# Streaming encoder trunk: one more row group of the first convolution projection in rounded products, and a new order at both FFN ends

## The chip, the core and the metric

One core of a Trainium2 chip runs the whole program. The metric is the device time of one launch in microseconds (us). The engines are TensorE (PE in the profile, its weight loads PEld), VectorE (DVE), ScalarE (ACT), GpSimd (POOL) and SyncE (SP). SP only issues transfers here; POOL issues those that add while they copy.

## What is computed

256 tokens of width 2048 pass through two layers: a Conformer convolution module with a SwiGLU FFN of width 5632, then multi-head latent attention with a second FFN, then a final RMSNorm.

```python
def conv_module(h, w_pw1, b_pw1, w_dw, b_dw, ln_g, ln_b, w_pw2, b_pw2):
    u = h @ w_pw1 + b_pw1                      # 2048 -> 4096
    a, gate = jnp.split(u, 2, axis=-1)
    v = a * jax.nn.sigmoid(gate)
    v = lax.conv_general_dilated(
        v, w_dw[:, None, :].astype(v.dtype), window_strides=(1,),
        padding=[(CONV_WIDTH - 1, 0)], dimension_numbers=('NWC', 'WIO', 'NWC'),
        feature_group_count=D_MODEL) + b_dw
    v = jax.nn.silu(layernorm(v, ln_g, ln_b))
    return v @ w_pw2 + b_pw2                   # 2048 -> 2048

def swiglu(h, w_gate, w_up, w_down):
    return (jax.nn.silu(h @ w_gate) * (h @ w_up)) @ w_down

def reference(...):
    ...
        h = h + y
        h = h + swiglu(rmsnorm(h, ffn_norm_g[i]), ffn_w_gate[i], ffn_w_up[i], ffn_w_down[i])
    return rmsnorm(h, final_norm_g)
```

Here `y` is the mixer's output for `rmsnorm(h, attn_norm_g[i])`, the convolution (31 taps, one filter a channel) in layer 0 and latent attention in layer 1.

Everything is float32. The kernel gets it in one of two ways. A plain float32 product is one instruction in the code and two records in the trace. A product "in three rounded terms" splits each operand into a rounded part (`_hi`, float32r) and the remainder (`_lo`): hi*hi + hi*lo + lo*hi, three fast matmuls.

## The kernel before

**Weights.** They come from HBM in groups of 1 MB: 512 rows (4 tiles of 128) by 512 columns. `raw`, `w_hi` and `w_lo` each have `RING = 4` slots; group `g` uses slot `g % 4`. ACT writes `w_hi` (a rounding copy, `hi`). The remainder is made in one of two ways: DVE subtracts (`lo`), or ACT writes `-raw` rounded into `w_lo` (`hi_and_negative`) and POOL issues a transfer that adds `raw` onto it (`conv_low`). A `raw` slot is loaded again when its last reader is done: PE (`group_used`) for a float32 group, the remainder (`lo_dve` or `lo_added`) for a rounded one. SP issues all loads in one queue, in program order.

**First projection and convolution** (`channel_half`, `conv_half`, `gate_sigmoid`, `products`, `conv_sums`, `conv_rows`). Eight halves `s = 0..7`, each 256 channels and their gates: four row groups `j`, each 4 tiles of rows by 4 tiles of columns (16 products of 128x128 weights by 256 tokens). `WHOLE = 2`: groups 0 and 1 are float32 products from `raw` and `x_f`; groups 2 and 3 are rounded, their remainders by `conv_low`. After a half, ACT takes the sigmoid of the gates (line 723), DVE multiplies (line 1086), and the 31 taps are shared: ACT makes 10 products (741) that POOL adds up (603), DVE does 21 steps for each of two channel tiles in turn (1101), and adds both sums (1107). In the last half ACT and POOL take 5 taps, DVE 14, and PE 12 with diagonal matrices (`diag_last`, made by ACT at line 712 after the first half's operands). `conv_rows` turns a finished half back to token rows. In the last half ACT also prepares the four groups of the second projection (`G_PW2`) before and between its gate sigmoid and its products. Layer norm, SiLU (`silu`) and the second projection (`square`) follow.

**FFN** (`ffn`). Eleven chunks of 512 hidden channels; from chunk 1 on a chunk has 15 groups of 1 MB, named `Q1 Q3 Q5 D0 D1 Q6 D2 Q7 D3 Q2 G2 Q4 G3 U2 U3` in this order, each with a position `q`. The `Q` groups are Strassen-like sums for half of gate and up, `G` and `U` plain ones, `D0..D3` the down projection of the chunk before. The last chunk's four down groups are `F_LAST + n`. `f_w(q)` names the `w_hi`/`w_lo` slot: `q % 4`, and `n` for `F_LAST + n`; `f_hi` on ACT waits until PE has used the group that had the slot last. With `F_LAST = 158` slot 0 was last used by position 156 and slot 1 by 157, before as after.

```python
            def f_hi(l, q):
                landed = 16 * (F_LAYER[f_raw(q), f_sum(q)] * l + F_LOADED[q])
                act.wait_ge(f_added[f_raw(q)] if f_sum(q) else f_in[f_raw(q)], landed)
                before = f_before(q, f_w)
                if before is not None:
                    wait_f_used(act, l, before)
```

At the end of a chunk DVE multiplies gate (`gate_mul`, 1258) and up (`up_mul`, 1268) into `ff_h`; PE transposes it (`hidden`, 1719); ACT and DVE split it (830, 1250) into `a_hi`, `a_lo`; then the down groups of that chunk may start. In all chunks but the last, that chain lies beside the next chunk's `Q` groups. Every engine works through its own list in order, so an instruction that waits holds up all that stand behind it.

Of the kernel before, what the change touches and what calls it, by code (L numbers as in the profile page):

```python
# [52 lines left out]
PE_TAPS_LAST = 12  # L53

# [5 lines left out]
WHOLE = 2  # L60
SPLIT = KG - WHOLE

# [16 lines left out]

G_ADDED = G_PW2 + RING  # L80
# [18 lines left out]
DOWN = (D0, D1, D2, D3)  # L99
F_CHUNK = 15  # L100
# [3 lines left out]
F_RAW = {Q1: 0, Q5: 0, Q6: 0, Q4: 0, Q3: 1, Q7: 1, D0: 4, D1: 2, D2: 3, D3: 4, Q2: 2, G2: 3, G3: 4, U2: 2, U3: 3}  # L104


def f_pos(c, p):
    return F_FIRST + F_CHUNK * (c - 1) + p


def f_part(q):
    return (q - F_FIRST) % F_CHUNK


def f_raw(q):

    if q < F_FIRST:
        return q % RING
    return F_RAW[f_part(q)] if q < F_LAST else q - F_LAST
# [61 lines left out]
def encoder(nc, x, positions, attn_norm_g, ffn_norm_g, final_norm_g, conv_w_pw1, conv_b_pw1, conv_w_dw,  # L181
# [3 lines left out]
    with ctx:  # L185
# [137 lines left out]
        glu_done = sem("glu_done")  # L323
        conv_step = sem("conv_step")
# [59 lines left out]

        def split_no(g):

            return SPLIT * (g // KG) + g % KG - WHOLE if g < G_PW2 else SPLIT * HALVES + g - G_PW2

        def wait_lo(eng, g, i=None, per=0):
            if KG <= g < G_ADDED:  # L390
                eng.wait_ge(lo_added[g % RING], 16 * (g // KG if g % KG >= WHOLE else 1))
            else:
                eng.wait_ge(lo_dve, val(split_no(g) + 1 if g < KG else SPLIT + g - G_ADDED + 1, i, per))
# [10 lines left out]
        def wait_f_used(eng, l, q):  # L404
            eng.wait_ge(f_used, F_ALL * l + q + 1)

# [44 lines left out]
        def _(sp):  # L451
# [50 lines left out]
            def ffn_loads(l):  # L502
# [23 lines left out]
                for c in range(1, FC):  # L526
                    for p in (D3, Q2, G2):
                        part(c, p)
                    if c < FC - 1:
                        part(c + 1, Q3)  # L530
                    for p in (G3, U2, U3):
                        part(c, p)
                    if c < FC - 1:
                        part(c + 1, Q1)
                        for p in (D0, D1, D2):
                            part(c + 1, p)
                for n in range(CC):
                    f_load(F_LAST + n, w_of(l, DOWN[n], FC))
            ffn_loads(0)
# [37 lines left out]
        def _(pool):  # L577
# [9 lines left out]
            def conv_low(g):  # L587

                slot = g % RING
                pool.wait_ge(neg_done, split_no(g) - SPLIT + 1)  # L590
                pool.dma_start(hi32(w_lo[:, slot, :]), raw[:, slot, :], accum_op=ALU.add).then_inc(lo_added[slot], 16)

            def conv_sums(s):
# [3 lines left out]
                for n in range(1, PROD_TAPS[s]):  # L597
                    pool.wait_ge(prod_done, 2 * (PROD_TAP[s] + n) + 2)
# [5 lines left out]
                    if n == 2 and s < HALVES - 1:  # L604
                        conv_low(G_PW1 + KG * (s + 1) + KG - 1)
# [51 lines left out]
        def _(act):  # L657
# [51 lines left out]
            act.wait_ge(vec_done, 3)  # L709
            for mm in range(2):  # L710
                for w in range(PE_TAPS_LAST):
# [3 lines left out]
            def gate_sigmoid(s):  # L715

                u = s % 2
                act.wait_ge(group_used, G_PW1 + KG * s + KG)
                if s >= 2:
                    act.wait_ge(glu_done, 2 * (s - 1))  # L720
                for mm in range(2):
                    col = KT + 2 * s + mm
                    act.activation(glu_sig[:, 2 * u + mm, :], ps[:, 2 * u + 1, S * mm:S * mm + S], ACT.Sigmoid,
                                   bias=bias1_col[:, col:col + 1]).then_inc(glu_sig_done, 1)

            def products(s, n0, n1):

                u = s % 2
                for n in range(n0, min(n1, PROD_TAPS[s])):
                    w = prod_tap0(s) + n  # L730
                    if n == 0 and s >= 2:
                        act.wait_ge(conv_tr, TT * (s - 1))
                    elif n > 0 and PROD_ADD[s] + n > PROD_SLOTS:
                        act.wait_ge(prod_added, PROD_ADD[s] + n - PROD_SLOTS)
                    elif n > 0:
                        act.wait_ge(out_added, TT)
                    for mm in range(2):
                        m, tile = 2 * u + mm, 2 * s + mm
                        act.wait_ge(glu_done, tile + 1)
                        dst = acc[:, m, :] if n == 0 else prod_slot(s, n)[:, S * mm:S * mm + S]  # L740
                        act.activation(dst, vbuf[:, m, w:w + S], ACT.Copy, scale=tap_col[:, w, tile:tile + 1]
                                       ).then_inc(prod_done, 1)
# [9 lines left out]
            for s in range(HALVES):  # L752
                g = G_PW1 + KG * (s + 1)
                if s == HALVES - 1:
                    hi_and_negative(g)
                    hi_and_negative(g + 1)
# [57 lines left out]
            def ffn(l):  # L814

                def gate_sig(c):

                    for t in range(TT):
                        if c > 0 and t == 0:
                            act.wait_ge(tile0_done, 2 * chunk_no(l, c) + 1)  # L820
                        else:
                            wait_f_used(act, l, KG - 1 if c == 0 else f_pos(c, G3))
# [3 lines left out]
                def hidden(c):  # L826

                    for b in range(2):
                        act.wait_ge(ff_tr, 2 * (FC * l + c) + b + 1)
                        act.activation(a_hi[:, 0, 2 * b:2 * b + 2, :].rearrange("p k s -> p (k s)"), ps[:, 4 + b, :],  # L830
                                       ACT.Copy).then_inc(ahi_done, 1)

                def parts_hi(c, *parts):
                    for p in parts:
                        f_hi(l, f_pos(c, p))

# [8 lines left out]
                for c in range(1, FC):  # L845
# [4 lines left out]
                    wait_f_used(act, l, f_pos(c, Q5))  # L850
# [1134 lines left out]
```

## Time and profile before

| | us |
|---|---|
| median of 3 runs | 2071.71 (2070.03 to 2072.25) |
| time of the profiled execution | 2071.21 |
| its span on the core | 2069.4 |
| TensorE busy in the span | 2010.9 (97%) |
| mean granted TensorE clock | 0.988 |

The span is what the trace shows; 1.8 us of the profiled time lie around it. In the rows further down, a row of the timeline gives start, duration, engine, line, operation, output and inputs, count, and in brackets the idle time before it and what ended it. PE works nearly all the time, so time can go in two ways only: less work for it, or fewer of the places where it stands still or runs at the lower clock.

### The profile page before, as it was taken

Reading aid. Unit: us, or ns where it says so; the run is one execution under the profiler, and the core shown is the slowest. Engines: PE = TensorE matmul, PEld = TensorE weight load, DVE = VectorE, ACT = ScalarE, POOL = GpSimd, SP = SyncE. Lnnn points to the kernel's source line nnn. Section 1 sums busy time; section 2 is a strip of 40 time slices with the busy share of each in tenths; the row PEclk is TensorE's granted clock in tenths of the full one; section 3 lists DMA queues with packets and bytes.
Section 4 is the critical chain, followed back from the end, with each engine's and each line's share of the span. In section 5 each row is a group of like instructions: output and inputs, shape, how many; then the busy total and the mean of one; then the engine's idle time right before and its main releaser. Section 6 shows DMA issues by size and latency. Waiting matters only on the chain.

```text
span 2069.4 us, 24296 instructions
## 1 busy us (share of the span) xinstructions
PE 2010.9 (97%) x9814; PEld 1705.5 (82%) x9814; DVE 1421.9 (69%) x1605; ACT 1054.8 (51%) x1020; POOL 226.1 (11%) x191
## 2 busy tenths in 40 slices
PE   8899899999999999999989999999999999999996
PEld 7898878888888888888878998888888888888885
DVE  4777676777766777667667775477766767766764
ACT  4566763545454555455445554355455445554543
POOL 0455400000000000000001000000000000000001
PEclk9999999999999999999999999999999999999998
DMA  7888946699889989898744534568988999889981
GB/s 234 240 227 234 263 143 214 169 279 258 227 224 259 268 267 236 216 260 245 243 143 138 158 122 160 191 177 270 251 217 240 253 274 262 224 227 262 263 244 61
DMA packets 254081, 457.51 MB, mean 221 GB/s; under 512 B 18452, under 2 KB 60188, under 8 KB 251164
## 3 DMA queue, kind: packets, MB, share of 16 engines
q1 hardware_dynamic: 207648, 349.73, 48.3%
q0 software_dynamic: 44832, 102.77, 28.7%
q10 hardware_dynamic: 1500, 3.61, 0.5%
q8 instruction: 71, 1.16, 0.2%
q14 instruction: 30, 0.25, 0.0%
HBM read 435.10 MB, written 2.10 MB: 211 GB/s over the span
## 4 chain that ended last, share of the span: by engine, by line
PE 85%; DVE 5%; DMA 5%; ACT 3%; issue 1%; POOL 0%; SPq 0%; ACTq 0%; DVEq 0%; POOLq 0%
PE ps L1496 82%; DVE w_lo L988 2%; DMA raw<-in_conv_w_pw_dram 2%; DMA w_lo<-raw 1%; DMA raw<-in_ffn_w_up_dram 1%; PE ps L1719 1%; POOL scratch L603 0%; PE ps L1920 0%; PE ps L1921 0%; PE ps L1901 0%; ACT w_hi L801 0%; DMA resid<-in_x_dram 0%; ACT w_lo L677 0%; ACT diag_last L712 0%; DVE x_lo L1015 0%
## 5 line engine op out<-in xcount | busy, mean ns | idle before, releaser
L988 DVE TENSOR_TENSOR w_lo<-raw,w_hi 128x2048 fp32r<-128x2048 f32 x264 | 601.5, 2287 | 279.0 <-ACT w_hi L801 278.7
L801 ACT ACTIVATE w_hi<-raw 128x2048 fp32r<-128x2048 f32 x264 | 500.9, 1914 | 488.3 <-PE ps L1496 197.1
L1496 PE MATMUL ps<-w_hi,x_hi 128*128 128x512 f32 x1328 | 517.9, 390 | 1.1 <-DVE x_lo L1015 0.9
L1496 PE MATMUL ps<-w_hi,x_lo 128*128 128x512 f32 x1328 | 516.7, 389 | 0.0
L1496 PE MATMUL ps<-w_lo,x_hi 128*128 128x512 f32 x1328 | 516.7, 389 | 0.0
L1496 PE MATMUL ps<-w_hi,a_hi 128*128 128x512 f32 (+1 forms) x768 | 294.5, 384 | 2.5 <-DVE a_lo L1250 2.5
L1496 PE MATMUL ps<-w_lo,a_hi 128*128 128x512 f32 (+1 forms) x768 | 293.9, 383 | 0.0
L1496 PEld LDWEIGHTS ps<-w_hi,x_hi 128*128 128x128 f32 x1328 | 249.3, 188 | 53.9 <-DVE x_lo L1015 1.4
L1496 PE MATMUL ps<-w_hi,a_lo 128*128 128x512 f32 (+1 forms) x768 | 293.6, 382 | 0.0
L1496 PEld LDWEIGHTS ps<-w_hi,x_lo 128*128 128x128 f32 x1328 | 249.3, 188 | 52.1
L1496 PEld LDWEIGHTS ps<-w_lo,x_hi 128*128 128x128 f32 x1328 | 249.3, 188 | 51.3
L622 POOL DMA_DIRECT2D raw<-in_ffn_w_up_dram x60 | 77.1, 1285 | 1255.1 <-DVE w_lo L988 1255.1
L672 ACT ACTIVATE w_hi<-raw 128x2048 fp32r<-128x2048 f32 x73 | 138.5, 1910 | 147.8 <-PE ps L1496 74.3
L1496 PEld LDWEIGHTS ps<-w_hi,a_hi 128*128 128x128 f32 x768 | 145.6, 190 | 31.7 <-DVE w_lo L988 3.5
L1496 PEld LDWEIGHTS ps<-w_hi,a_lo 128*128 128x128 f32 x768 | 145.6, 190 | 28.0
L1496 PEld LDWEIGHTS ps<-w_lo,a_hi 128*128 128x128 f32 x768 | 145.6, 190 | 27.7
L801 ACT ACTIVATE w_hi<-row_bc 128x2048 fp32r<-128x2048 f32 x60 | 115.2, 1919 | 92.7 <-PE ps L1496 92.7
L983 DVE TENSOR_TENSOR w_lo<-raw,w_hi 128x2048 fp32r<-128x2048 f32 x55 | 125.5, 2291 | 40.8 <-ACT w_hi L672 40.6
L988 DVE TENSOR_TENSOR w_lo<-row_bc,w_hi 128x2048 fp32r<-128x2048 f32 x60 | 137.0, 2284 | 4.6 <-ACT w_hi L801 4.5
L1496 PE MATMUL ps<-w_hi,s_hi 128*128 128x512 f32 x320 | 126.4, 395 | 0.0
L1496 PE MATMUL ps<-w_hi,s_lo 128*128 128x512 f32 x320 | 124.8, 390 | 0.0
L1496 PE MATMUL ps<-w_lo,s_hi 128*128 128x512 f32 x320 | 124.5, 389 | 0.0
(210 smaller groups left out, 2323.8 us busy)
## 6 DMA issues: line engine op xcount, KB each, us to landing
raw<-in_ffn_w_gate_dram SPq DMA_DIRECT2D x68, 1024.0 KB, 9.5
raw<-in_ffn_w_up_dram SPq DMA_DIRECT2D x68, 1024.0 KB, 7.5
raw<-in_ffn_w_up_dram POOLq DMA_DIRECT2D x60, 1024.0 KB, 9.0
raw<-in_ffn_w_down_dram SPq DMA_DIRECT2D x48, 1024.0 KB, 6.0
row_bc<-in_ffn_w_down_dram SPq DMA_DIRECT2D x40, 1024.0 KB, 8.8
raw<-in_conv_w_pw_dram SPq DMA_DIRECT2D x64, 512.0 KB
raw<-in_ffn_w_gate_dram POOLq DMA_DIRECT2D x20, 1024.0 KB, 9.8
row_bc<-in_ffn_w_gate_dram SPq DMA_DIRECT2D x20, 1024.0 KB, 6.4
```

What stands on the lines that cost most here:

```text
L622: pool.dma_start(f_raw_tile(l, q).rearrange("p (k n) -> p k n", k=GK), w_of(l, p, c), accum_op=ALU.add).then_inc(f_added[f_raw(q)], 16)
L672: act.activation(w_hi[:, slot, :], raw[:, slot, :], ACT.Copy).then_inc(hi_done, 1)
L801: act.activation(f_w_tile(w_hi, l, q), f_raw_tile(l, q), ACT.Copy).then_inc(f_hi_done, 1)
L983: dve.tensor_tensor(w_lo[:, g % RING, :], raw[:, g % RING, :], hi32(w_hi[:, g % RING, :]), ALU.subtract).then_inc(lo_dve, 1)
L988: dve.tensor_tensor(f_w_tile(w_lo, l, q), f_raw_tile(l, q), hi32(f_w_tile(w_hi, l, q)), ALU.subtract).then_inc(f_lo_done, 1)
L1496: ins = pe.matmul(dst, lhsT, rhs, start=first and n == 0, stop=last and n == len(pairs) - 1, skip_group_check=skip)
L1719: ins = pe.transpose(ps[:, 4 + b, S * kk + P * t:S * kk + P * t + P], ff_h[:, t, P * m:P * m + P], ident[:, :])
```

## The change

1. `WHOLE` goes from 2 to 1: row group 1 of each half is rounded too. Its remainder is made by DVE (`lo`), right after the half's two gate multiplications; groups 2 and 3 keep `conv_low` (`ADDED_FROM = 2`). The second projection's first four groups (`G_PW2 + 0..3`) get their remainders by DVE too, one before the SiLU steps and three between them.
2. The load of group 1 no longer waits for PE's use of it but for its remainder. ACT prepares group 1, then group 2, takes the sigmoids, and then prepares group 3 ahead of its products; POOL issues both adding transfers ahead of its sums. `diag_last` is made four matrices at a time after the products of halves 1 to 6. ACT loads its Sigmoid table early.
3. In the last half PE finishes channel tile 0 and its gates (`last_tile0`), then tile 1; ACT and DVE take tile 0, then tile 1, in that order.
4. In the last FFN chunk the order is `Q6 Q2 Q7 G2 G3 Q4 U2 U3 D2 D3`: two down groups of the chunk before come last, and `hidden` stands between them. SP's order follows. `a_hi`/`a_lo` of the last chunk use another slot and the transposes other PSUM banks.

```diff
-WHOLE = 2
+WHOLE = 1
+ADDED_FROM = 2
+ORDER_LAST = (Q1, Q3, Q5, D0, D1, Q6, Q2, Q7, G2, G3, Q4, U2, U3, D2, D3)
...
             for s in range(HALVES):
-                if s == HALVES - 1:
-                    for j in range(WHOLE):
-                        conv_low(G_PW2 + j)
-                    conv_low(G_PW2 + WHOLE)
-                else:
-                    conv_low(G_PW1 + KG * (s + 1) + WHOLE)
+                if s < HALVES - 1:
+                    for j in range(ADDED_FROM, KG):
+                        conv_low(G_PW1 + KG * (s + 1) + j)
                 conv_sums(s)
-            conv_low(G_PW2 + KG - 1)
...
+            for s in range(HALVES - 1):
                 g = G_PW1 + KG * (s + 1)
+                hi(g + 1)
                 hi_and_negative(g + 2)
-                gate_sigmoid(s)
+                for mm in range(2):
+                    gate_sigmoid(s, mm)
+                hi_and_negative(g + 3)
                 products(s, 0, 3)
-                hi_and_negative(g + 3)
                 if s > 0:
                     rows_out(s - 1)
-                products(s, 3, TAPS)
+                products(s, 3, PROD_TAPS[s])
+                if s > 0:
+                    last_diagonals(s - 1)
+            for mm in range(2):
+                gate_sigmoid(HALVES - 1, mm)
+                for n in range(PROD_TAPS[HALVES - 1]):
+                    product_of(HALVES - 1, n, mm)
+                if mm == 0:
+                    hi(G_PW2)
+            rows_out(HALVES - 2)
+            for j in range(1, KG):
+                hi(G_PW2 + j)
             rows_out(HALVES - 1)
...
@@ DVE, conv_half @@
+                if last:
                     for mm in range(2):
+                        gated(mm)
+                        for w in range(w0, TAPS):
+                            tap(w, mm)
+                else:
+                    gated(0)
+                    gated(1)
+                    lo(G_PW1 + KG * (s + 1) + WHOLE)
+                    for w in range(w0, TAPS):
+                        tap(w, 0)
+                        tap(w, 1)
...
@@ PE, channel_half @@
+                    elif j == ADDED_FROM:
+                        channel_products(s, j, (0, 2))
+                    else:
+                        channel_products(s, j, (0, 2)).then_inc(last_tile0, 1)
+                        channel_products(s, ADDED_FROM, (1, 3)).then_inc(group_used, 1)
+                        channel_products(s, j, (1, 3)).then_inc(group_used, 1)
...
@@ SP, last chunk of the FFN @@
+                c = FC - 1
+                for p in (G2, G3, U2):
+                    part(c, p)
+                last_down(1)
+                part(c, U3)
+                last_down(0)
+                part(c, D2)
+                part(c, D3)
+                last_down(2)
+                last_down(3)
...
@@ ACT, last chunk @@
+                        parts_hi(c, Q6, Q2, Q7, G2)
+                        q167_out(c)
+                        parts_hi(c, G3, Q4, U2, U3)
+                        gate_sig(c)
+                        parts_hi(c, D2, D3)
+                        f_hi(l, f_next(c, 0))
...
+                    f_hi(l, f_next(c, 1))
+                    if c < FC - 1:
+                        f_hi(l, f_next(c, 2))
                 hidden(FC - 1)
...
@@ DVE, last chunk @@
+                        parts_lo(c, G3, Q4, U2, U3)
+                        gate_mul(c)
+                        parts_lo(c, D2, D3)
+                        f_lo(l, f_next(c, 0))
+                        up_mul(c)
+                        f_lo(l, f_next(c, 1))
+                        hidden(c)
+                        add(2, f_pos(c, D2))
+                        f_lo(l, f_next(c, 2))
+                        add(3, f_pos(c, D3))
+                        f_lo(l, f_next(c, 3))
...
@@ PE, last chunk @@
+                        q2(c)
+                        q7(c)
...
+                        plain(c, G2, 0, 2, q167_done)
+                        plain(c, G3, 0, 3)
+                        strassen(c, Q4, 1, x_tile(1, 1))
+                        pe.wait_ge(mixed, 4 * n + 4)
                     plain(c, U2, 2, 2)
                     plain(c, U3, 2, 3)
+                    if c == FC - 1:
+                        down(c - 1, 2, f_pos(c, D2))
+                        hidden(c)
+                        down(c - 1, 3, f_pos(c, D3))
```

`f_next(c, n)` is the position `n` places after the end of chunk `c`; behind the last chunk that is `F_LAST + n`. `q7` waits for the second of DVE's three mixing steps (lines 1301 to 1306), which itself needs `Q6` done by PE.

## Rows read from the trace of the kernel before

**Rows 1.** The page, part 1: busy us, share of the span, instructions.
```profile
PE 2010.9 (97%) x9814; PEld 1705.5 (82%) x9814; DVE 1421.9 (69%) x1605; ACT 1054.8 (51%) x1020; POOL 226.1 (11%) x191
```
**Rows 2.** The chain that ended last, in time order: start us, us, what.
```profile
42.21 3.31 ACT diag_last L712 x11
...
57.95 11.41 DMA w_lo<-raw
...
230.17 18.50 DMA raw<-in_conv_w_pw_dram
...
1040.47 1.92 ACT w_hi L801
```
**Rows 3.** Timeline of PE, an undisturbed half of the projection.
```profile
84.76 7.07 PE L1496 MATMUL ps<-x_f,raw 128*128 128x256 f32 x32
...
91.79 0.28 PE L1496 MATMUL ps<-x_lo,w_hi 128*128 128x256 f32 x1
...
103.05 0.28 PE L1496 MATMUL ps<-x_hi,w_lo 128*128 128x256 f32 x1
```
**Rows 4.** Timeline of PE, the two longest stops of the projection.
```profile
69.40 0.58 PE L1496 MATMUL ps<-x_hi,w_hi 128*128 128x256 f32 x1 [4.82 <-DMA w_lo<-raw]
...
77.41 0.81 PE L1496 MATMUL ps<-x_f,raw 128*128 128x256 f32 x3
...
203.85 0.43 PE L1496 MATMUL ps<-x_hi,w_hi 128*128 128x256 f32 x1 [1.97 <-DMA w_lo<-raw]
```
**Rows 5.** Busy by stretch, core 0: no transfer, an adding one alone, loads alone.
```profile
104.00:106.00 2.00, 2.00 (x11) 1.74 (x11) 0.00 (x0) 2.00 (x2) 0.00 (x0) 1.00 0.04 14
...
110.00:112.00 2.00, 2.00 (x13) 1.77 (x12) 2.00 (x7) 2.00 (x3) 1.86 (x2) 1.00 1.00 197
126.00:128.00 2.00, 2.00 (x20) 2.00 (x18) 0.51 (x2) 0.00 (x0) 0.00 (x0) 1.00 1.11 349
```
**Rows 6.** Transfers issued in 100 to 164 us: KB, median us to landing.
```profile
w_lo<-raw POOLq DMA_DIRECT2D x5, 1024.0 KB, 8.2
```
**Rows 7.** Timelines of ACT and of DVE in the same halves.
```profile
129.75 1.91 ACT L672 ACTIVATE w_hi<-raw 128x2048 fp32r<-128x2048 f32 x1 [9.47 <-DMA raw<-in_conv_w_pw_dram]
...
108.78 15.76 DVE L1101 SCALAR_TENSOR_TENSOR ps<-scratch,tap_col,ps 128x256 f32<-128x256 f32 x40
```
**Rows 8.** Timelines behind the last half: PE, then DVE, then ACT.
```profile
241.21 12.58 PE L1496 MATMUL ps<-diag_last,scratch 128*128 128x128 f32 x96 [3.65 <-DVE scratch L1086]
257.32 1.16 PE L1496 MATMUL ps<-ident,scratch 128*128 128x128 f32 x8 [3.53 <-DVE scratch L1107]
...
269.90 0.47 PE L1496 MATMUL ps<-w_hi,x_hi 128*128 128x512 f32 x1 [0.20 <-DVE x_lo L1152]
...
242.27 10.27 DVE L1101 SCALAR_TENSOR_TENSOR ps<-scratch,tap_col,ps 128x256 f32<-128x256 f32 x26
256.52 0.75 DVE L1107 TENSOR_TENSOR scratch<-scratch,ps 128x256 f32<-128x256 f32 x2 [3.98 <-POOL scratch L603]
...
248.69 1.91 ACT L672 ACTIVATE w_hi<-raw 128x2048 fp32r<-128x2048 f32 x1 [5.03 <-DMA raw<-in_conv_w_pw_dram]
```
**Rows 9.** Timelines at the first FFN's end: PE, then ACT, then DVE.
```profile
1046.08 1.97 PE L1719 MATMUL ps<-ident,scratch 128*128 128x128 f32 x8 [5.71 <-DVE scratch L1268]
1048.97 0.77 PE L1496 MATMUL ps<-w_hi,a_hi 128*128 128x512 f32 x1 [0.92 <-DVE a_lo L1250]
...
1054.11 0.40 PE L1496 MATMUL ps<-w_hi,a_hi 128*128 128x512 f32 x1
...
1035.03 1.92 ACT L801 ACTIVATE w_hi<-raw 128x2048 fp32r<-128x2048 f32 x1 [11.68 <-PE ps L1496]
...
1036.98 2.29 DVE L988 TENSOR_TENSOR w_lo<-raw,w_hi 128x2048 fp32r<-128x2048 f32 x1 [11.31 <-ACT w_hi L801]
...
1044.62 1.40 DVE L1268 SCALAR_TENSOR_TENSOR scratch<-ps,rstd,scratch 128x512 f32<-128x512 f32 x2
```
**Rows 10.** Last chunks: DVE's second mixing step in either layer, and PE behind Q6.
```profile
1002.69 0.69 DVE L1304 TENSOR_TENSOR scratch<-scratch,ps 128x512 f32<-128x512 f32 x1
...
1988.07 0.69 DVE L1304 TENSOR_TENSOR scratch<-scratch,ps 128x512 f32<-128x512 f32 x1
...
999.41 0.39 PE L1496 MATMUL ps<-w_hi,a_hi 128*128 128x512 f32 x1
```
**Rows 11.** Timeline of PE, the second FFN's end.
```profile
2032.77 1.97 PE L1719 MATMUL ps<-ident,scratch 128*128 128x128 f32 x8 [5.71 <-DVE scratch L1268]
```

More of the change, by code:

```diff
@@ L118, in f_raw @@
         return q % RING
-    return F_RAW[f_part(q)] if q < F_LAST else q - F_LAST
+    if q >= F_LAST:
+        return q - F_LAST
+    return (F_RAW_LAST if in_last(q) else F_RAW)[f_part(q)]
 def f_w(q):
@@ L744, in rows_out @@
+            def products(s, n0, n1):
+                for n in range(n0, n1):
+                    for mm in range(2):
+                        product_of(s, n, mm)
             def rows_out(s):
@@ new lines, in conv_half, with gated @@
+                w0 = dve_tap0(s)
+                steps = TAPS - w0
+                bank = [ps[:, 6 + u, S * mm:S * mm + S] for mm in range(2)]
+                def gated(mm):
+                    tile = 2 * s + mm
+                    dve.wait_ge(glu_sig_done, tile + 1)
+                    dve.scalar_tensor_tensor(vbuf[:, 2 * u + mm, HALO:], ps[:, 2 * u + mm, 0:S],
+                                             bias1_col[:, tile:tile + 1], glu_sig[:, 2 * u + mm, :],
+                                             ALU.add, ALU.mult).then_inc(glu_done, 1)
@@ new lines, in tap @@
+                def tap(w, mm):
+                    m, tile = 2 * u + mm, 2 * s + mm
+                    if w == w0:
+                        dve.wait_ge(glu_done, tile + 1)
+                        dve.tensor_scalar(bank[mm], vbuf[:, m, w:w + S], tap_col[:, w, tile:tile + 1],
+                                          vec_col[:, R_BDW + tile:R_BDW + tile + 1],
+                                          ALU.mult, ALU.add).then_inc(conv_step, 1)
+                        return
+                    dve.wait_ge(conv_step, DVE_STEP[s] + (steps * mm + w - w0 if last else 2 * (w - w0) + mm - 1))
+                    dve.scalar_tensor_tensor(bank[mm], vbuf[:, m, w:w + S], tap_col[:, w, tile:tile + 1],
+                                             bank[mm], ALU.mult, ALU.add).then_inc(conv_step, 1)
@@ L1105, in conv_half @@
                     dve.wait_ge(prod_added, PROD_ADD[s + 1])
-                    dve.wait_ge(conv_step, DVE_STEP[s] + 2 * (TAPS - w0) + mm - 1)
+                    dve.wait_ge(conv_step, DVE_STEP[s] + (steps * (mm + 1) if last else 2 * steps + mm - 1))
                     dve.tensor_tensor(acc[:, m, :], acc[:, m, :], bank[mm], ALU.add).then_inc(conv_step, 1)
@@ new lines, in channel_products @@
+            def channel_products(s, j, tiles):
+                slot = (G_PW1 + KG * s + j) % RING
+                w, wh, wl = w_rows(raw, slot), w_rows(w_hi, slot), w_rows(w_lo, slot)
+                for kk in range(GK):
+                    k = GK * j + kk
+                    for m in tiles:
+                        cols = slice(P * m, P * m + P)
+                        if j < WHOLE:
+                            pairs = [(w[:, kk, cols], x_f[:, k, :])]
+                        else:
+                            pairs = [(wh[:, kk, cols], x_hi[:, k, :]), (wh[:, kk, cols], x_lo[:, k, :]),
+                                     (wl[:, kk, cols], x_hi[:, k, :])]
+                        ins = product(ps[:, 2 * (s % 2) + m % 2, S * (m // 2):S * (m // 2) + S], pairs,
+                                      k == 0 and m < 2, k == KT - 1, skip=True)
+                return ins
@@ L1785, in ffn @@
                     chunk(c)
-                hidden(FC - 1)
                 def between(n):
```

286 lines of the change are left out of this document (149 added, 137 removed).

## The prediction, as it was made before the change was run

> **What bounds the kernel now.** The page first: PE is busy for 97% of the span [rows 1], so what counts is PE's work and its few stops. The chain of waits says where these are [rows 2]: ACT's diagonal matrices at 42 us stand ahead of an adding transfer that lands at 69.4 us; a load takes the chain behind the last half (230 us); and at 1040 us ACT's rounding copy begins a stop at the end of the first FFN. The second FFN ends the same way [rows 11]. The timeline of PE gives their sizes. All else that the change touches is hidden today.
>
> The two products, from an undisturbed half [rows 3]. 32 records of a float32 row group (16 products) take 7.07 us, 0.221 us each; with two records to a product that is 0.44 us. From the record at 91.79 us to the one at 103.05 us are 94 steps, 0.120 us each, so a product in three rounded terms takes 0.36 us. A group is 7.06 us in float32 and 5.75 us rounded.
>
> **Part 1, row group 1 rounded.** 1.3 us less for PE in each of eight halves: -10.4 us. The page "FP8 and Floating Point Precision" of the Trainium skill (TensorE Precision Notes) counts a true float32 product as four passes. The row agrees in kind, but a fourth of 0.44 us is 0.11 us and the rounded matmul takes 0.12; by passes alone the gain would be 14 us. The rows decide.
>
> What it adds: a rounding copy on ACT (1.91 us [rows 7]) and a subtraction on DVE (2.29 us, the same size at [rows 9]) in each half. The half will last 7.06 + 3 x 5.75 + 0.45 for the transposes = 24.8 us. DVE's share is now 15.8 us of taps [rows 7] and some 3.4 us around them; with 2.3 us it is 21.5 of 24.8. ACT gets to about 20 us. Neither bounds. But DVE's subtraction stands behind the two gate multiplications, which wait for the sigmoids: by my count it ends 4 us after PE begins the next half, and PE wants it at 7. Cover 3 us; each us beyond that is paid once a half.
>
> **Part 2, loads and adds sooner.** PE stops twice for an adding transfer [rows 4]. At 69.4 us it stood 4.82 us, after a first stop of 1.46 us, and then took 8.01 us (69.40 to 77.41) for 48 rounded records that take 5.75: the granted clock in that stretch was 0.50, the lower of its two levels. With it 8.5 us. At 203.85 us it is 1.97 us and 1.6 us more from the same clock, 3.6 us. A third stop is 0.5 us. Together 12.6 us. Do they go? The first comes from the 24 diagonal matrices ahead of the group's rounding copy on ACT [rows 2]; these now follow in six lots of four behind the products, where ACT has 4 us a half free.
>
> The others come from transfers. An adding transfer is on its way for 8.2 us [rows 6] and by itself keeps all 16 DMA engines full, at 197 GB/s [rows 5]; at that it works 5.3 us. Loads run at 349 GB/s [rows 5]: 4.2 MB, 12 us a half. So a half needs 12 + 2 x 5.4 = 23 us of DMA, out of 26 us now and 24.8 after. It fits if the DMA is never left without work; now it is for 4 us around 105 us [rows 5], since three of the four loads queue behind the one that waits for PE's group 1. After, group 1's load follows group 0's at once, 7 us into the half instead of 14. Then group 2's data land about 20 us into the half, not at its end as now (ACT waits for them at 129.75 us, when PE begins the next half [rows 7]); its add is issued at 24 and lands by 7 us into the next half, where PE wants it at 13. Group 3: ACT at 1 to 4.7 us, landed at 12 to 13, wanted at 19. Both have 6 us in hand. I take all 12.6 us as gone. Bounds: 3 us of them stay, or all but the first stop's 8.5.
>
> So PE ends the last half 10.4 + 12.6 = 23.0 us sooner.
>
> **Part 3, behind the last half.** Call PE's end of that half E (237.1 now). Now ACT prepares groups of the second projection first, the sigmoids begin at E + 3, DVE's 26 tap steps run to 252.5, and a load that lands late (248.69, after 5.03 us of waiting) holds ACT's last products, so POOL's sums are in at 256.5 and PE ends the rows at 258.5 = E + 21.4 [rows 8]. After: tile 0 is complete at E - 5.7, but DVE comes from half 6 only at E - 2.4. Each tap step then follows one on the same data; a step lasts 0.48 us (the 26 go at 0.39 because two tiles alternate), so with 0.03 us for the hand-over 14 steps take 7.3 us. Tile 0 is done at E + 5.5, tile 1 at E + 13.4, the sums at E + 14.2, the rows at E + 15.5. ACT and POOL end before that (E + 8 and E + 12); PE's 96 diagonal records (12.58 us [rows 8], partly at the lower clock) end at about E + 13. Gain 5.9 us; if the serial steps ran at 0.39 us, PE's diagonals would bind and it were 7; if DVE came 2 us later, 4.
>
> The layer norm is unchanged: 11.4 us until the second projection starts at 269.90. In its first block DVE now has three subtractions of 2.3 us between its SiLU steps, 1.4 us of DVE work for 2.7 us of PE's; one of them holds up the second pair of operands. I take 0.5 us lost (0 to 2).
>
> Sum for the convolution: 23.0 + 5.9 - 0.5 = **28.4 us gained**.
>
> **Part 4, the FFN ends.** Now: PE ends U3 at 1040.2. The rounding copy of F_LAST + 1 waits for that, DVE's subtraction follows, and only behind it comes up_mul (to 1046.02) [rows 9]. The down projection starts at 1048.97, 8.8 us after U3; its first 12 matmuls take 5.14 us (to 1054.11) where 12 take 2.72 at full clock. Now read the new lists in order. DVE has f_lo(F_LAST + 0) *ahead of* up_mul. That needs f_hi(F_LAST + 0), and slot 0 was last used by position 156, which is now D2. So up_mul waits for PE's D2. PE: U3 ends, D2 runs 5.45 us; then ACT 0.25 + 1.92 us, DVE 2.25 us, the same two steps as today [rows 9], up_mul 1.40 us: PE stands for 5.8 us ahead of the transposes, as long as now, but 5.45 us later. Then the transposes (1.97 us at the lower clock) and D3 (5.45 us and about 1 for the clock). Behind D3 it comes again: ACT has f_hi(F_LAST + 1), which waits for slot 1, position 157, D3, *ahead of* its hidden copies; DVE has the subtraction ahead of its own. ACT 0.25 + 1.92, DVE 2.25 for the subtraction, 1.28 for the two a_lo, 0.65 for the first block of add(2), which PE's first block now waits for: 6.4 us of standing. From U3's end to the start of the last down projection: 5.45 + 5.8 + 2.0 + 6.5 + 6.4 = 26.2 us, of which 10.9 are the two down groups that came from earlier. 15.3 against 8.8: **6.5 us lost**, in each layer. The work queued behind these waits is all that is left in the layer, so nothing covers them.
>
> One more: with D2 gone from between Q6 and Q7, only Q2 (2.72 us) covers DVE's mixing. In the first layer Q6 ends at 999.4, Q2 would at 1002.1, the second step ends at 1003.4 [rows 10]: 1.3 us. In the second layer it ends at 1988.8 as Q2 does: 0. Loads are no term: each is issued more than 10 us ahead of its use.
>
> FFN ends: -6.5 x 2 - 1.3 = **14.3 us lost** (bounds 8 to 20, by how the clock answers; below in a rival, a gain).
>
> **Sum.** 2071.2 (profiled) - 28.4 + 14.3 = 2057.1; the median of the runs is 0.5 us above that execution: 2057.6, **2058 us**. With the terms' own bounds (convolution 21 to 31, ends 8 to 20) 2049 to 2070.
>
> **Rivals.** (a) *The FFN ends do what their place suggests*: the chain of waits lies beside D2 and D3, and the stop of 5.71 + 0.92 us, the slow transposes (1.1) and the slow first matmuls (2.4) go in each layer [rows 9, 11]: 10.1 x 2. For it: 10.9 us of work stand there, the chain is 9. Against: slots and list order as above. It would give 2071.7 - 28.4 - 20.2 = 2023.
> (b) *DMA bounds the halves.* 23 us of transfers in 24.8, with each in a queue behind a wait. If halves 2 to 7 stay at 26.1 us and the stop in half 6 stays: 6 x 1.3 + 3.6 = 11.4 us back, 2069. For it: DMA shares of 0.9 and more in that stage. Against: its idle 4 us are now filled.
> (c) *Slower than before.* The add of group 2 or 3 comes too late more often. Place: PE at row group 2 of a half. It decides from 6 us beyond the 8.2 us from issue to landing. Each such stop costs like the one at 69.4 us, 8.5 us with its clock. Two cost 17 and bring the time to 2075; three, 2083. For it: at 57.95 us an add took 11.4 us, beside the loads that now come at the same time as group 3's add. Against: 6 us in hand and only 3 shown.
> (d) *It doesn't do what it says*: the convolution's end stays on DVE (serial steps, late start), 5.9 us come to nothing: 2064, inside the range.
>
> **Chances.** Forecast, with (d) in it, 0.72 (2049 to 2067); (a) 0.08; (b) 0.13; (c) 0.07. The range is 2046 to 2070: it takes in the forecast with its bounds and (b), and leaves out (a) and (c). What this kernel's measurement can tell from no change is about 0.2%, 4.1 us. (b) lies within it, (c) beyond it. Faster 0.83, same 0.11, slower 0.06.
>
> **What the changed profile would show.** The halves: PE from one float32 group to the next in 24.8 us, no idle time at w_lo, granted clock 1.00 from 20 us to E near 214. Second projection from about 241.5 us. At both FFN ends: *two* stops of PE, 5 to 7 us each, the one ahead of line 1719's counterpart ended by up_mul, the one ahead of the last down projection ended by DVE's resid or a_lo; ACT's rounding copy begins 0.25 us after D2 and after D3. Wrong would be: one stop or none there, PE waiting for w_lo in more than one half, or DVE still at tap steps when PE has long ended the diagonals by more than 2 us.

## The result and the profile after

| | before | after |
|---|---|---|
| median, us | 2071.22 (2069.95 to 2075.1, 6 runs) | 2078.82 (2075.33 to 2081.2, 6 runs) |
| span of the profiled execution, us | 2069.4 | 2078.6 |
| mean granted TensorE clock | 0.988 | 0.987 |

The ratio is 1.003, with an interval of 1.0016 to 1.0044: the change makes the kernel 0.3% slower, some 7 us. The prediction was 2058 (2046 to 2070), faster.

The page of the changed kernel, part 1, answers to [rows 1]: PE has 4.2 us less to do, the span is 9.2 us longer, so PE stands still for 13.4 us more.
```profile
PE 2006.7 (97%) x9942; PEld 1705.6 (82%) x9942; DVE 1451.8 (70%) x1619; ACT 1064.0 (51%) x1027; POOL 223.1 (11%) x187
```
The timeline of PE in the changed kernel's first projection, answering to [rows 3, 4]: a float32 group at the start of the third half, then its stops up to the second projection. In brackets is the idle time and what ended it.
```profile
68.51 7.07 PE L1600 MATMUL ps<-x_f,raw 128*128 128x256 f32 x32
...
77.05 0.39 PE L1600 MATMUL ps<-x_hi,w_hi 128*128 128x256 f32 x1 [1.03 <-DVE w_lo L1051]
91.92 0.39 PE L1600 MATMUL ps<-x_hi,w_hi 128*128 128x256 f32 x1 [3.09 <-DMA w_lo<-raw]
...
132.34 0.38 PE L1600 MATMUL ps<-x_hi,w_hi 128*128 128x256 f32 x1 [0.96 <-DVE w_lo L1051]
147.38 0.38 PE L1600 MATMUL ps<-x_hi,w_hi 128*128 128x256 f32 x1 [3.27 <-DMA w_lo<-raw]
...
201.83 0.39 PE L1600 MATMUL ps<-x_hi,w_hi 128*128 128x256 f32 x1 [3.12 <-DMA w_lo<-raw]
209.16 7.07 PE L1600 MATMUL ps<-x_f,raw 128*128 128x256 f32 x32
229.91 0.58 PE L1600 MATMUL ps<-x_hi,w_hi 128*128 128x256 f32 x1 [4.61 <-DMA w_lo<-raw]
...
240.50 10.88 PE L1600 MATMUL ps<-diag_last,scratch 128*128 128x128 f32 x96
...
263.99 0.47 PE L1600 MATMUL ps<-w_hi,x_hi 128*128 128x512 f32 x1 [1.43 <-DVE x_lo L1236]
```
The long stop at 69 us [rows 4] is gone. In its place the third, fifth and seventh half stop for a group's adding transfer by 3 us each, and the last by 4.6. In the third and the fifth PE also waits 1 us for DVE's subtraction of group 1. PE ends the last half at 240.2 us (237.1 before). The second projection still begins sooner, at 263.99 us (269.90 in [rows 8]).

The FFN ends, same view, answering to [rows 9, 11]: two stops in each layer where one stood.
```profile
1037.09 1.97 PE L1840 MATMUL ps<-ident,scratch 128*128 128x128 f32 x8 [5.71 <-DVE scratch L1354]
1052.27 0.77 PE L1600 MATMUL ps<-w_hi,a_hi 128*128 128x512 f32 x1 [6.23 <-DVE resid L1362]
...
2030.00 1.97 PE L1840 MATMUL ps<-ident,scratch 128*128 128x128 f32 x8 [5.71 <-DVE scratch L1354]
2045.35 0.77 PE L1600 MATMUL ps<-w_hi,a_hi 128*128 128x512 f32 x1 [6.23 <-DVE resid L1362]
```
The last down projection of the first layer begins at 1052.27 us against 1048.97, though the layer began 5.0 us sooner: 8.3 us lost. In the second it is 2045.35 against 2035.66 from a start 2.4 us later: 7.3. So the profiled execution reads: convolution 5.0 gained, ends 15.6 lost, 0.9 gained in between, 9.7 us later in all.

### The profile page after: what moved, and what is told of

Same layout as the page of the kernel before. It is cut to its first block, busy times and chain, and to the rows that moved or that the text cites. A ratio compares the mean times of both kernels' runs of the same rounds, so it can differ in the third digit from the quotient of the medians.

```text
span 2078.6 us, 24648 instructions
## 1 busy us (share of the span) xinstructions
PE 2006.7 (97%) x9942; PEld 1705.6 (82%) x9942; DVE 1451.8 (70%) x1619; ACT 1064.0 (51%) x1027; POOL 223.1 (11%) x187
## 4 chain that ended last, share of the span: by engine, by line
PE 82%; DMA 6%; DVE 6%; ACT 2%; issue 2%; SPq 1%; POOL 0%; ACTq 0%; DVEq 0%; POOLq 0%
PE ps L1600 79%; DVE w_lo L1056 3%; DMA w_lo<-raw 2%; DMA raw<-in_conv_w_pw_dram 2%; DMA raw<-in_ffn_w_up_dram 1%; SPq L515 1%; PE ps L1840 1%; ACT w_hi L852 1%; PE ps L2062 0%; PE ps L2063 0%; PE ps L2043 0%; ACT w_lo L710 0%; DMA resid<-in_x_dram 0%; DVE x_lo L1083 0%; PE ps L1639 0%
## 5 line engine op out<-in xcount | busy, mean ns | idle before, releaser
L1056 DVE TENSOR_TENSOR w_lo<-raw,w_hi 128x2048 fp32r<-128x2048 f32 x264 | 601.5, 2288 | 291.7 <-ACT w_hi L852 291.5
L852 ACT ACTIVATE w_hi<-raw 128x2048 fp32r<-128x2048 f32 x264 | 500.4, 1914 | 488.9 <-PE ps L1600 211.0
L705 ACT ACTIVATE w_hi<-raw 128x2048 fp32r<-128x2048 f32 x81 | 153.6, 1912 | 130.3 <-PE ps L1600 73.4
L1051 DVE TENSOR_TENSOR w_lo<-raw,w_hi 128x2048 fp32r<-128x2048 f32 x67 | 152.9, 2290 | 38.7 <-ACT w_hi L705 38.4
L1600 PEld LDWEIGHTS ps<-w_lo,a_hi 128*128 128x128 f32 x768 | 146.2, 190 | 27.6
L1600 PE MATMUL ps<-x_hi,w_hi 128*128 128x256 f32 (+1 forms) x400 | 117.3, 293 | 16.2 <-DMA w_lo<-raw 14.1
```

What stands on the lines that cost most here:

```text
L705: act.activation(w_hi[:, slot, :], raw[:, slot, :], ACT.Copy).then_inc(hi_done, 1)
L852: act.activation(f_w_tile(w_hi, l, q), f_raw_tile(l, q), ACT.Copy).then_inc(f_hi_done, 1)
L1051: dve.tensor_tensor(w_lo[:, g % RING, :], raw[:, g % RING, :], hi32(w_hi[:, g % RING, :]), ALU.subtract).then_inc(lo_dve, 1)
L1056: dve.tensor_tensor(f_w_tile(w_lo, l, q), f_raw_tile(l, q), hi32(f_w_tile(w_hi, l, q)), ALU.subtract).then_inc(f_lo_done, 1)
L1600: ins = pe.matmul(dst, lhsT, rhs, start=first and n == 0, stop=last and n == len(pairs) - 1, skip_group_check=skip)
```

## The experiments

Two questions: does the loss lie in the FFN ends, as the steps of the prediction say, and why did the convolution gain so little? Against my forecast for the halves (all stops go) stands its rival: the transfers set their length. Ratios are to the kernel before, measured on the same chip. The changed kernel was not measured again beside the experiments, so a number of us "below the changed kernel" compares medians of different occasions; worked out from the ratios, the two such numbers (33 and 17) would be 2 us larger.

**The two parts apart.** The hunks of the convolution alone, without those of the FFN.

> The kernel before with parts 1 to 3 of the change (the convolution) and the FFN as it was. The two traces say that both FFN ends cost 8.3 and 7.3 us and the convolution gives some 6 us at the start of the second projection. If that split is right: 2078.8 - 15.6 = 2063 us, 0.4% faster than before, with no stop at either FFN end but those of before (down projection 8.8 us after U3). Rival, that the FFN's loss is a consequence of an earlier, shifted start and not of its order: 2075 or more.

Measured: 2062.15 us, ratio 0.9943 (0.992 to 0.9965). That is 11.8 us gained by the ratio (7 to 17), where I had forecast 28.4. PE stops for an adding transfer in the third half and in the fifth to the eighth, for example
```profile
88.86 0.58 PE L1533 MATMUL ps<-x_hi,w_hi 128*128 128x256 f32 x1 [2.89 <-DMA w_lo<-raw]
...
227.35 0.38 PE L1533 MATMUL ps<-x_hi,w_hi 128*128 128x256 f32 x1 [4.50 <-DMA w_lo<-raw]
```
PE ends the last half at 237.6 us, as late as in the kernel before (237.1), and the second projection begins at 261.51 us against 269.90: what the profiled execution gains up to there, it gains behind the last half, and nothing in the halves.

The hunks of the FFN alone:

> The kernel before with the change's FFN hunks alone (order of the last chunk's parts, the two ends); the convolution is untouched. Theory: the new ends cost 8.3 and 7.3 us and nothing else in these hunks matters, so 2071.2 + 15.6 = 2087 us, within 2084 to 2090, and the same stops of 5.7 and 6.2 us stand in both ends. Rival: the ends are dear only because of where the shortened convolution leaves the loads; then it comes out below 2080.

Measured: 2088.19 us, ratio 1.0081 (1.0061 to 1.0101), 16.8 us lost. The two stops have the same size here, where the convolution is the old one; PE in its first layer:
```profile
1043.97 1.97 PE L1789 MATMUL ps<-ident,scratch 128*128 128x128 f32 x8 [5.71 <-DVE scratch L1317]
1059.11 0.77 PE L1563 MATMUL ps<-w_hi,a_hi 128*128 128x512 f32 x1 [6.22 <-DVE resid L1325]
```
0.9943 x 1.0081 = 1.0024, within the interval of the whole change: as far as these intervals tell, the parts add up and don't meet.

**The order in the two lists at the FFN's end.** The prediction said that the loss is not in moving the down groups but in what stands ahead of what on ACT and DVE. So only that is turned (DVE, then ACT); with it one `add` moves up a place:
```diff
                         parts_lo(c, D2, D3)
+                        up_mul(c)
                         f_lo(l, f_next(c, 0))
-                        up_mul(c)
-                        f_lo(l, f_next(c, 1))
                         hidden(c)
                         add(2, f_pos(c, D2))
+                        f_lo(l, f_next(c, 1))
+                        add(3, f_pos(c, D3))
                         f_lo(l, f_next(c, 2))
-                        add(3, f_pos(c, D3))
                         f_lo(l, f_next(c, 3))
...
-                    f_hi(l, f_next(c, 1))
                     if c < FC - 1:
+                        f_hi(l, f_next(c, 1))
                         f_hi(l, f_next(c, 2))
                 hidden(FC - 1)
-                for n in (2, 3):
+                for n in (1, 2, 3):
```


> The changed kernel with two pairs turned in the last FFN chunk: DVE does up_mul ahead of f_lo(F_LAST + 0) and hidden ahead of f_lo(F_LAST + 1), ACT does hidden ahead of f_hi(F_LAST + 1). Theory (the stops come from the order of the lists, slot 0 and 1 being D2's and D3's): both stops of 5.7 and 6.2 us go, the transposes take 0.9 us instead of 2.0 and the matmuls behind them run at full clock; down projection at once behind D3. 2078.8 - 15.6 - 20.2 = 2043 us. Rival (the loads or the PSUM banks bind there): at least one stop of 4 us or more stays, 2060 or more.

Measured: 2045.78 us, ratio 0.9861 (0.9836 to 0.9887), 33 us below the changed kernel. DVE's timeline, then PE's transposes, which now have nothing idle ahead of them:
```profile
1019.85 0.74 DVE L1354 SCALAR_TENSOR_TENSOR scratch<-ps,rstd,scratch 128x512 f32<-128x512 f32 x1
1022.50 0.75 DVE L1354 SCALAR_TENSOR_TENSOR scratch<-ps,rstd,scratch 128x512 f32<-128x512 f32 x1 [1.91 <-PE ps L1600]
1029.95 2.29 DVE L1056 TENSOR_TENSOR w_lo<-raw,w_hi 128x2048 fp32r<-128x2048 f32 x1 [6.70 <-ACT w_hi L852]
...
1027.75 1.03 PE L1840 MATMUL ps<-ident,scratch 128*128 128x128 f32 x8
```
up_mul runs at 1019.9 and 1022.5 us, beside D2, and the subtraction for the next group comes 7 us later. The chain was always short enough; two waits for a slot stood in front of it. Of the 33 us, 15.6 are the loss that is undone; the rest is what the new place of D2 and D3 is worth, 8.7 us a layer (10.1 in rival (a)).

**Half of each adding transfer.** If the adds hold up PE and nothing else does, smaller ones must set it free. The remainders of groups 2 and 3 are added for half of the columns only; the other half gets no add.
```diff
-                pool.dma_start(hi32(w_lo[:, slot, :]), raw[:, slot, :], accum_op=ALU.add)
+                pool.dma_start(hi32(w_lo[:, slot, 0:GK * CH // 2]), raw[:, slot, 0:GK * CH // 2], accum_op=ALU.add)
```


> The changed kernel, but each adding transfer moves only the first half of its columns (the remainders of groups 2 and 3 are then wrong in the other half; all instructions, waits and orders stay). Theory (transfers bind the halves: two adds and four loads run beside each other, an add takes 13.7 us, and between two halves the DMA engines have nothing to do for 4 us): DMA work of a half falls from 23 to 18 us, the stops at w_lo go, a half takes 24.8 us, PE ends the last half at 217 us or sooner instead of 240; 2056 us. Rival (the new order on ACT and POOL, or DVE's subtraction behind the sigmoids, makes the stops): PE still stops at w_lo in three or more halves, end of the last half 232 or later, 2070 or more.

Measured: 2057.43 us, ratio 0.9916 (0.9893 to 0.994). No stop for w_lo is left, and a half lasts 24.6 us:
```profile
189.24 7.07 PE L1600 MATMUL ps<-x_f,raw 128*128 128x256 f32 x32
...
213.86 0.60 PE L1739 MATMUL ps<-ident,scratch 128*128 128x128 f32 x4
```
PE ends at 214.0 us, which is the forecast for the change itself. So PE's and DVE's terms were right. Of the 26.2 us between the two kernels (240.2 against 214.0), 23.9 stand in the third, fifth, seventh and eighth half: 14.1 in the four stops for an add, 2.0 in the two for DVE's subtraction, some 6.3 in the low clock behind the adds' stops, the rest in smaller gaps. The other 2.3 stand in the first half: in the profiled execution of the changed kernel the granted clock was 0.50 from 19 to 21 us, with half adds 1.00. The code of the first half is the same in both, so I take this for a matter of the execution and not of the change.

**One adding transfer fewer, nothing left out.** DVE makes the remainder of group 2 as well, and one adding transfer is left in a half (the groups that PE takes in turn in the last half stay the same).
```diff
-ADDED_FROM = 2
+ADDED_FROM = 3
+TURN_FROM = 2
...
-                hi_and_negative(g + 2)
+                hi(g + 2)
...
                     lo(G_PW1 + KG * (s + 1) + WHOLE)
+                    lo(G_PW1 + KG * (s + 1) + WHOLE + 1)
```


> The changed kernel with group 2's remainder made by DVE as well (one adding transfer a half instead of two, no negative copy for it, 2.3 us more DVE work a half, so 23.8 of 24.8 us). Theory (transfers bind): halves of 25 us, end of the last half at 218 to 222 us, 2058 us. Rival (DVE or the chain through the sigmoids binds): PE stops ahead of group 1 or 2 for a subtraction in most halves, halves of 26 us or more, 2066 or more.

Measured: 2061.81 us, ratio 0.9939 (0.9915 to 0.9963), 17 us below the changed kernel; 3.8 above what I expected. Seven halves have no stop, the last has one, whose add ran beside the loads of the second projection (the chain of waits, then PE):
```profile
196.63 13.47 DMA w_lo<-raw
...
210.14 0.58 PE L1602 MATMUL ps<-x_hi,w_hi 128*128 128x256 f32 x1 [4.88 <-DMA w_lo<-raw]
```

**Are the sooner loads at fault?** At first this looked likely, since adds beside loads are slow. The load of each half's second group is held again until PE is through with that group:
```diff
+                    elif g >= RING and j == 1:
+                        wait_lo(sp, g - RING)
+                        sp.wait_ge(group_used, g - RING + 1)
```


> The changed kernel, with the load of each half's second group held again until TensorE is through with that group, as in the kernel before (about 12 us later in a half); the remainders stay as in the change. Theory one (the cycle of loads, high part, negative and adding transfers is the bound, and a later load only starts it later): no faster than the changed kernel, stops in more halves, 2079 to 2095 us. Theory two (the sooner loads are the fault, because they run beside the adding transfers of the same groups): the stops go and it comes to 2065 us or less.

Measured: 2081.79 us, ratio 1.0049 (1.0032 to 1.0066). Theory two falls, as far as this edit tests it: in the fourth half SP issues the group's load at 112.4 us instead of 107.5, 5 us later and not 12, since in the changed kernel it gets to it only 8 us into the half. The stops stand in the same halves:
```profile
91.70 0.39 PE L1603 MATMUL ps<-x_hi,w_hi 128*128 128x256 f32 x1 [2.68 <-DMA w_lo<-raw]
...
146.84 0.43 PE L1603 MATMUL ps<-x_hi,w_hi 128*128 128x256 f32 x1 [3.05 <-DMA w_lo<-raw]
...
230.16 0.58 PE L1603 MATMUL ps<-x_hi,w_hi 128*128 128x256 f32 x1 [4.89 <-DMA w_lo<-raw]
```
And the held group reaches ACT's copy at 67.00 us, against 66.79 in the changed kernel. That fits DMA engines that have work in that time either way: in the changed kernel their mean share is 1.0 from 75 to 98 us. Issuing this load 5 us sooner or later does not move the round of transfers.

**The diagonals alone.** The kernel before, with its 24 diagonal matrices made four at a time at the end of halves 1 to 6.
```diff
+            def last_diagonals(part):
+                for n in range(4 * part, 4 * part + 4):
...
                 products(s, 3, TAPS)
+                if 0 < s < HALVES - 1:
+                    last_diagonals(s - 1)
```


> The kernel before with one edit: the 24 diagonals of the last channel tiles are made by ScalarE four at a time at the end of halves 1 to 6, not all before the first sigmoid. Theory: the stop of 4.8 us in the second half goes and the later stop of the kernel before stays, so 2071.2 - 4.8 = 2066.4 us. Rival: without it the add or the sigmoid of the next half is late instead, as in the changed kernel: within 1 us of the kernel before.

Measured: 2065.17 us, ratio 0.9971 (0.9961 to 0.9981). PE's stop in the second half is 1.29 us and not 4.82 [rows 4], and the slow clock behind it is gone too. The stop of the fourth half grows from 0.49 to 2.03 us, with a granted clock of 0.50 from 119 to 121 us behind it. Together the halves end 5 us sooner, and the time is 6.0 us lower by the ratio:
```profile
64.20 0.38 PE L1500 MATMUL ps<-x_hi,w_hi 128*128 128x256 f32 x1 [1.29 <-DMA w_lo<-raw]
...
118.15 0.39 PE L1500 MATMUL ps<-x_hi,w_hi 128*128 128x256 f32 x1 [2.03 <-DMA w_lo<-raw]
```

**All of it together.** The turned ends, one add in a half, and the second projection's first four loads held until the last add has landed:
```diff
                 if in_float32(g - RING):
                     sp.wait_ge(group_used, g - RING + 1)
+                    wait_lo(sp, G_PW2 - 1)
+                elif G_PW2 <= g < G_PW2 + KG:
+                    wait_lo(sp, g - RING)
+                    wait_lo(sp, G_PW2 - 1)
```


> The changed kernel with three edits: the FFN ends turned (as in the earlier run with that alone), group 2's remainder by DVE so that one adding transfer is left in a half, and the second projection's first four loads held until the last adding transfer of the convolution has landed. Theory: the three are independent. Ends 33 us below the changed kernel, one add 17 us, and the last half's stop of 4.9 us goes since the add at 196.6 us then moves alone and takes about 8 us and not 13.5: 2078.8 - 33 - 17 - 4.9 = 2024 us. Rival: the held loads make the second projection late by more than the stop that goes: 2029 us or more. If the ends and the halves share a cause, the sum is not reached: above 2035 us.

Measured: 2029.18 us, ratio 0.9795 (0.9779 to 0.9812): 42 us below the kernel before, the fastest version here. The held loads did what was expected of them in the last half: its add is the transfer issued in 198 to 216 us (KB, us to landing), and it lands after 7.6 us instead of 13.47.
```profile
w_lo<-raw POOLq DMA_DIRECT2D x1, 1024.0 KB, 7.6
```
In the profiled execution a stop appeared one half earlier, where the add was issued 7.8 us into the half and took 13.27 us beside loads (chain, then PE):
```profile
174.66 13.27 DMA w_lo<-raw
...
187.98 0.39 PE L1606 MATMUL ps<-x_hi,w_hi 128*128 128x256 f32 x1 [2.13 <-DMA w_lo<-raw]
```
In the kernel with one add and no held loads the same add, issued as far into the half, landed in 10.6 us. Why it is 13 us in one execution and under 11 in the other is open.

The number is that of the rival, 2029 and not 2024, but its mechanism isn't what the trace shows. The second projection does begin later, at 248.11 us against 244.21 with one add and no held loads, yet no engine waits for the held loads: ACT's copies of them follow its other work without idle time. What ends the convolution is DVE. Its last sums begin at 230.83 us with one add and at 234.70 here, 3.9 us apart as the second projections are; DVE (first two lines), then PE, in each case one add first:
```profile
230.83 0.74 DVE L1192 TENSOR_TENSOR scratch<-scratch,ps 128x256 f32<-128x256 f32 x2
234.70 0.75 DVE L1196 TENSOR_TENSOR scratch<-scratch,ps 128x256 f32<-128x256 f32 x2
...
244.21 0.47 PE L1602 MATMUL ps<-w_hi,x_hi 128*128 128x512 f32 x1 [1.47 <-DVE x_lo L1238]
248.11 0.47 PE L1606 MATMUL ps<-w_hi,x_hi 128*128 128x512 f32 x1 [0.39 <-DVE x_lo L1242]
```
In both kernels DVE goes from the taps of the seventh half to those of the last one without idle time. So the stop of 4.88 us at 210 us stood beside DVE's work and held up next to nothing, and the 4.9 us that I had put down for its end did not come: 2078.8 - 33 - 17 = 2028.8 is about what came out, give or take the few us by which the occasions differ. The profiled execution is itself the slowest of its four, 4 us above the median; 2.3 us of that stand in its first half, at the low clock (0.50 from 19 to 21 us), so the stop at 187.98 us need not be in the others.

## Why the prediction was wrong

**FFN ends: right.** Two stops per layer, 5.71 and 6.23 us (forecast 5.8 and 6.4), the first ended by up_mul, the second by DVE's resid; ACT's rounding copies 0.25 us behind PE; 0.93 us behind Q6 and Q2 (1.3). The cost in the trace was 15.6 us, alone 16.8, forecast 14.3.

**PE's work and the tail: right or better.** A half without stops takes 24.6 us (24.8 forecast). Behind the last half, a tap step of a single tile takes 6.79 us for 13, 0.52 each (0.51). The rows end 12.4 us after PE's E, not 15.5: PE had stood still at 225 to 230 us while DVE went on, so DVE came in time. With half adds, where nothing stopped, it was 14.4. From E to the second projection it is 23.8 us, 32.8 before: 9.0 gained for a forecast of 5.4. Without PE's stop it would be less, 7.0 by the 25.8 us of the run with half adds, so some of it is luck: the stop in the halves, paid there, let DVE catch up.

**The step that failed is part 2:** "It fits if the DMA is never left without work", then "group 2's data land about 20 us into the half" and "Both have 6 us in hand. I take all 12.6 us as gone." What it led to, PE ending the last half 23.0 us sooner, came out as 3.1 us later. In the changed kernel's third half (68.51 us) ACT's timeline shows where group 2's data really land:
```profile
66.79 1.91 ACT L705 ACTIVATE w_hi<-raw 128x2048 fp32r<-128x2048 f32 x1 [7.00 <-DMA raw<-in_conv_w_pw_dram]
69.81 1.91 ACT L705 ACTIVATE w_hi<-raw 128x2048 fp32r<-128x2048 f32 x1 [1.11 <-DMA raw<-in_conv_w_pw_dram]
71.63 1.89 ACT L710 ACTIVATE w_lo<-raw 128x2048 fp32r<-128x2048 f32 x1
```
The copy at 66.79 us is of group 1, 22.5 us into its half (from 44.33). Group 2 comes at 69.81, when the next half has begun: 25 us, not 20. Then follow the copy, the negative and the issue of the add at 73.82 us, 5.5 us later than I had it, and group 3's at 78.15, 9.6 us into the half where I had some 5. Most of the 6 us in hand was gone before an add was issued. The rest went in group 3's add: 13.72 us from issue to landing, where I had reckoned with 8.2. It landed at 91.87 us, and PE had wanted it at 88.83. The chain of waits of the changed kernel shows one whole round:
```profile
53.13 4.68 SPq L515
57.86 0.73 SPq L515
58.63 11.16 DMA raw<-in_conv_w_pw_dram
69.84 1.79 issue
71.63 1.90 ACT w_lo L710
73.82 0.86 POOL w_lo L630
74.68 3.45 issue
78.15 13.72 DMA w_lo<-raw
```
A load lands, ACT copies and negates, POOL adds, and only behind the adds can slots 2 and 3 be loaded again. While ACT does its part, nothing is left to move; the DMA share (the last but one number) falls to nothing in each half, first in the changed kernel, then in the kernel before:
```profile
72.00:74.00 2.00, 2.00 (x11) 1.77 (x10) 0.08 (x1) 2.00 (x3) 0.18 (x1) 1.00 0.00 2
100.00:102.00 2.00, 2.00 (x11) 1.77 (x10) 0.55 (x2) 2.00 (x4) 0.65 (x1) 1.00 0.03 8
...
106.00:108.00 2.00, 2.00 (x11) 1.77 (x10) 0.91 (x3) 1.68 (x4) 0.87 (x1) 1.00 0.00 0
132.00:134.00 2.00, 2.00 (x12) 1.74 (x10) 0.08 (x1) 2.00 (x3) 0.25 (x1) 1.00 0.03 9
```
I had put that gap of 4 us down to loads queued behind a wait for PE, and taken it for filled. It is the turn from load to add, and the change leaves it. So a half needs 23 us of transfers *and* 4 of turning. POOL's timeline says it without any sum, by the time from one half's first add to the next: changed kernel, then kernel before.
```profile
101.35 0.87 POOL L630 DMA_DIRECT2D w_lo<-raw  x1 [9.09 <-ACT w_lo L710]
129.11 0.87 POOL L630 DMA_DIRECT2D w_lo<-raw  x1 [9.23 <-ACT w_lo L710]
...
106.93 0.87 POOL L591 DMA_DIRECT2D w_lo<-raw  x1 [10.81 <-ACT w_lo L677]
133.75 0.87 POOL L591 DMA_DIRECT2D w_lo<-raw  x1 [8.69 <-ACT w_lo L677]
159.81 0.87 POOL L591 DMA_DIRECT2D w_lo<-raw  x1 [7.90 <-ACT w_lo L677]
```
Over all halves the round is 27.6 us in the changed kernel (46.10 to 211.46, six rounds) and PE's halves 27.5 (44.33 to 209.16). In the kernel before it was 26.7 over the last four (106.93 to 213.72), while an undisturbed half of PE was 26.0. It is 27.5 with the loads held, 27.0 with the diagonals alone moved; with half adds 24.3, about PE's pace, and with one add 25.0. By this the transfers bound these halves already, hidden by the fact that PE ran ahead for some halves and paid in one stop. Making PE's half 1.3 us shorter could bring nothing, as the convolution's hunks alone show (last half ended at 237.6 us, 237.1 before): the saving turned into more stops, each with the low clock behind it (the 48 records from 91.92 us to the next half at 99.26 take 7.3 us, not 5.75).

Rival (b) had this mechanism and the wrong price: it let the halves fall back to 26.1 us, PE's own pace of before, not to the 27.5 of the round. Rival (c) had the form in which it shows, late adds in several halves, and its times, 2075 and 2083, stand around the measured 2079. It got 7% because of the 6 us in hand. Put in, the sum comes right. The second projection begins at 263.99 us and not at the forecast 241.5, 22.5 later (26.2 in the halves, 2.3 of them the first half's low clock, less 3.7 behind them); 0.9 us more are lost in its first block, 1.3 more at the ends, and 0.9 are gained between: 2057.1 + 22.5 + 0.9 + 1.3 - 0.9 = 2080.9 for a profiled execution, whose span was 2078.6 with some 1.8 around it.

That leaves one thing unexplained: why the round grew from 26.7 us to 27.6. All four stops stand behind a second add of the half that took 13.7 to 14.1 us; the other three took 9.6 or 9.7, and the last five of the kernel before 8.9 to 9.7. Up to the seventh half the slow ones are those issued 8.7 to 9.6 us into the half, behind the loads of groups 0 and 1; the others were issued 6.1 to 6.4 us into it, ahead of them; the last half's, issued at 6.6, has the second projection's loads beside it. The page "DMA: Bandwidth & Descriptors" of the Trainium skill (Issuing engines are not separate DMA queues) says that transfers share the 16 engines whoever issues them and interleave; the 13 to 14 us of such an add against 7.6 with the loads held agree. But holding a load back by 5 us changed the round by 0.1 us only, so this isn't shown to be the cause of the longer round.

## What to carry to other kernels

Where a ring of buffers goes from load to compute to an adding transfer and back to load, measure the round in the trace (from one round's issue to the next) and put it beside PE's own undisturbed time; the engines' idle time in the turn belongs to the round. If the round is longer, a shorter PE stage only moves its stops, and the cure is to take a transfer out of the round. In a list written by hand, a copy into a slot is also a wait for the slot's last reader: when the work before it is reordered, put what the next stage waits for ahead of that copy.

## What the runs showed of the hardware

- An adding transfer of 1 MB within SBUF took 7.6 us from issue to landing with the loads held back. In the changed kernel a half's first add took 7.1 to 8.5 us, its second 9.6 to 14.1, with 13.7 or more wherever PE stood still for it; the median of all 14 was 9.0. The prediction had reckoned with 8.2, and 11.4 at most.
- SP's issue of a load was slow at times: group 1's second half-load took 4.68, 5.03 and 5.24 us in three halves of the chain, each time with an add on its way, where the two or three issues ahead of it took 0.4 to 0.7.
- The granted clock fell behind a stop, and not at once: after the 3.09 us that ended at 91.92 it was 1.00 up to 93 us and 0.50, the lower level of 1.2 GHz, from 94 to 96, so the 48 records took 7.3 us against 5.75. Behind the stop of 1.29 us (diagonals alone) it stayed at 1.00. Of two stops of equal length it fell behind one (2.03 us, diagonals alone, 0.50 from 119 to 121 us) and stayed at 1.00 behind the other (2.04 us at 170.91, convolution alone), so the length of the stop by itself doesn't tell. One stretch of the first:
```profile
94.00:95.00 1.00, 1.00 (x7) 1.00 (x6) 0.88 (x3) 0.66 (x1) 0.00 (x0) 0.50 1.10 347
```
